# Router logits with the turned tokens as stationary operand, and the experts' scatter as two fp32r products

## The reference

```python
g_logits = xt @ wg + bg                       # xt = RMSNorm(h); 4 groups
e_logits = (xt @ we + be).reshape(n_tok, 4, 8)
e_in = e_logits[tok, argmax(g_logits)]        # 8 experts of the chosen group
top_v, top_i = top_k(e_in, 2)
top_w = softmax(top_v) * g_prob[tok, g_sel]
for e in range(32):
    out += combine[:, e] * ((silu(xt @ w1[e]) * (xt @ w3[e])) @ w2[e])
```

## Time and profile before

| | |
|---|---|
| median of 3 runs | 417.2 us (416.52 to 417.85) |
| the profiled execution | 416.37 us, its span 414.6 us |
| mean granted clock of TensorE | 0.991 |
| PE, PEld busy | 388.9, 269.0 us |
| DVE, ACT, POOL busy | 176.9, 145.4, 12.8 us |
| moved by DMA | 139.88 MB, 337 GB/s over the span |

### The profile page before, as it was taken

The page is one execution under the profiler, slowest core; times in us unless marked ns, Lnnn a source line. Parts: engine busy times, 40 slices in busy tenths (PEclk is TensorE's granted clock), DMA queues, the critical chain, the costliest instruction groups (busy, mean ns, idle before and its releaser), DMA issues.

```text
span 414.6 us, 7327 instructions
## 1 busy us (share of the span) xinstructions
PE 388.9 (94%) x2990; PEld 269.0 (65%) x2990; DVE 176.9 (43%) x340; ACT 145.4 (35%) x285; POOL 12.8 (3%) x33
## 2 busy tenths in 40 slices
PE   7999999999999999999989999999989999979783
PEld 5999988767777777788865555545354646445342
DVE  3847674999898685784263010010102010100203
ACT  6834442638565635442221122121221212211033
POOL 3001000300000000000010000000000000000000
PEclk9999999999999999999999999999999999999897
DMA  8999999643441597569997999999999999999972
GB/s 297 420 417 345 390 397 363 261 152 108 147 154 62 192 344 269 191 243 403 427 419 251 418 430 430 428 411 428 427 427 427 428 428 430 427 428 424 425 326 103
DMA packets 17310, 139.88 MB, mean 337 GB/s; under 512 B 2176, under 2 KB 2560, under 8 KB 5632
## 3 DMA queue, kind: packets, MB, share of 16 engines
q1 hardware_dynamic: 16416, 138.60, 83.0%
q10 hardware_dynamic: 864, 0.84, 0.6%
HBM read 138.38 MB, written 1.05 MB: 336 GB/s over the span
## 4 chain that ended last, share of the span: by engine, by line
PE 47%; issue 46%; DVE 5%; POOL 1%; ACT 0%; POOLq 0%; DVEq 0%
PE bank L1545 5%; PE bank L1547 4%; PE bank L1546 4%; PE bank L1403 4%; PE bank L1404 4%; PE bank L1405 4%; PE bank L1668 2%; PE bank L1666 2%; PE bank L1667 2%; PE bank L1507 1%; PE bank L1533 1%; PE bank L1519 1%; PE bank L1388 1%; PE bank L1565 1%; PE bank L1465 1%
## 5 line engine op out<-in xcount | busy, mean ns | idle before, releaser
L1781 PE MATMUL bank<-ring,kv 128*32 128x512 f32 x512 | 64.1, 607 | 6.9 <-DMA ring<-in_experts 3.9
L464 DVE TENSOR_TENSOR part<-ring,part 128x2048 fp32r<-128x2048 f32 (+1 forms) x26 | 57.4, 2213 | 18.7 <-ACT part L457 18.7
L457 ACT CAST part<-ring 128x2048 fp32r<-128x2048 f32 (+1 forms) x26 | 48.0, 1847 | 31.2 <-DMA ring<-in_front 31.1
L1321 DVE TENSOR_TENSOR kv<-bank,prm 128x512 f32<-128x512 f32 x8 | 5.5, 692 | 109.4 <-PE bank L1749 109.4
L1749 PEld LDWEIGHTS bank<-qcur,h 128*128 128x128 f32 x256 | 32.3, 194 | 28.4 <-issue 28.4
L1749 PE MATMUL bank<-qcur,h 128*128 128x128 f32 x256 | 39.8, 293 | 0.0
L1545 PE MATMUL bank<-part,xhi 128*128 128x512 f32 x96 | 39.2, 408 | 0.0
L1821 PE MATMUL bank<-ring,hidT 128*32 128x256 f32 (+1 forms) x640 | 35.2, 342 | 3.2 <-DMA ring<-in_experts 2.7
L1831 PE MATMUL bank<-gab,vbd 128*128 128x256 f32 (+1 forms) x160 | 36.3, 359 | 1.4 <-ACT gab L911 1.3
L1547 PE MATMUL bank<-part,xlo 128*128 128x512 f32 x96 | 37.6, 391 | 0.0
L1546 PE MATMUL bank<-part,xhi 128*128 128x512 f32 x96 | 37.5, 390 | 0.0
(11 more groups left out here) (243 smaller groups left out, 532.6 us busy)
## 6 DMA issues: line engine op xcount, KB each, us to landing
ring<-in_experts SPq DMA_DIRECT2D x31, 2048.0 KB, 30.9
ring<-in_experts SPq DMA_DIRECT2D x32, 1024.0 KB, 8.4
ring<-in_front SPq DMA_DIRECT2D x28, 1024.0 KB, 5.7
ring<-in_front SPq DMA_DIRECT2D x4, 512.0 KB, 6.9
ring<-in_projs SPq DMA_DIRECT2D x4, 512.0 KB, 5.1
ring<-in_experts SPq DMA_DIRECT2D x4, 512.0 KB, 31.1
ring<-in_front SPq DMA_DIRECT2D x2, 560.0 KB, 8.9
h<-in_x SPq DMA_DIRECT2D x2, 512.0 KB, 3.8
```

The lines of the kernel that those rows point to most:

```text
L457: nc.scalar.copy(high(n, half)[:, 0:c].bitcast(F32R), raw(n, half)[:, 0:c]).then_inc(hi_done, 1)
L464: nc.vector.tensor_tensor(low(n, half)[:, 0:c].bitcast(F32R), raw(n, half)[:, 0:c], high(n, half)[:, 0:c], ALU.subtract).then_inc(split_do ...
L1781: ins = mm(bank[0][CAP * e:CAP * (e + 1)], xgT[:, q, CAP * e:CAP * (e + 1)], expert(j, q, e), start=(q == 0), stop=(q == NQ1 - 1))
```

## The change

The router's product swaps its operands: the turned tokens are stationary (128 columns), the router's 40 real columns move, and the logits come out by token in bank 3 at once. The copy `lgT`, the constant `fold2`, and their semaphores go. All four squares must be done before the first of these matmuls.

The scatter becomes two fp32r matmuls with a stationary operand of zeros and ones: the weight `share` is put on the rows of the second product by ACT, as the high part, and DVE makes the low part, `ylo` (five more instructions a block). DVE's copy of `cmbT` becomes a comparison and a sum. Piece 4 of the second product goes to bank 1. In the tail, the order of second products and scatters changes, DVE takes one of ACT's six squares, and POOL makes the factor of each token tile by itself.

```diff
@@ router, PE
-            pe.wait_ge(ssq_done, NT + 1)
+            pe.wait_ge(ssq_done, NT + 4)
             for k in range(KT):
                 pe.wait_ge(h2T_done[k // 4], 2)
-                ins = mm(bank[0][HD * (k % 2):HD * (k % 2) + HD, 0:T], rw[:, k], h2T[k // 2][:, (k % 2) * T:(k % 2 + 1) * T], start=(k < 2), stop=(k >= KT - 2))
-            ins.then_inc(lgT_full, 1)
-
-            pe.wait_ge(lgT_done, 1)
-            pe.wait_ge(ssq_done, NT + 4)
-            for t in range(NT):
-                ins = mm(bank[3][:, t * RC:(t + 1) * RC], lgT[:, t * P:(t + 1) * P], fold2, start=True, stop=True)
+                for t in range(NT):
+                    ins = mm(bank[3][:, t * RC:(t + 1) * RC], h2T[k // 2][:, (k % 2) * T + t * P:(k % 2) * T + (t + 1) * P], rw[:, k, 0:RC],
+                             start=(k == 0 and t == 0), stop=(k == KT - 1 and t == NT - 1))
             ins.then_inc(logit_full, 1)
@@ router, ACT
-            act.wait_ge(lgT_full, 1)
-            nc.scalar.copy(lgT, bank[0][:, 0:T]).then_inc(lgT_done, 1)
@@ blocks, ACT and DVE
-                nc.scalar.copy(yN[:, columns(p)], second_out(p, slice(0, P))).then_inc(yn_done, 1)
+                nc.scalar.activation(yN[:, columns(p)].bitcast(F32R), second_out(p, slice(0, P)), ACT.Copy, scale=share).then_inc(yn_done, 1)
-                nc.vector.tensor_copy(cmbT, bank[1][:, 0:T]).then_inc(cmb_done, 1)
+                nc.vector.tensor_scalar(cmbT.bitcast(F32R), bank[1][:, 0:T], 0.0, None, ALU.is_gt)
+                nc.vector.tensor_reduce(share, bank[1][:, 0:T], AX.X, ALU.add).then_inc(cmb_done, 1)
@@ blocks, DVE, at the end of through(b)
+                for p in range(NP):
+                    dve.wait_ge(yn_done, b * NP + (p + 1) + 1)
+                    dve.wait_ge(comb_done, b * NP + (p - 2 + 1 + NP))
+                    nc.vector.scalar_tensor_tensor(low_out(p).bitcast(F32R), second_out(p, slice(0, P)), share, yN[:, columns(p)],
+                                                   ALU.mult, ALU.subtract).then_inc(ylo_done, 1)
@@ blocks, PE, combine(p)
+                        pe.wait_ge(ylo_done, b * NP + (p + 1))
                         for t in range(NT):
-                            ins = mm(sum_of_piece(t, p), cmbT[:, t * P:(t + 1) * P], yN[:, columns(p)],
+                            onehot = cmbT[:, t * P:(t + 1) * P].bitcast(F32R)
+                            mm(sum_of_piece(t, p), onehot, yN[:, columns(p)].bitcast(F32R), start=False, stop=False)
+                            ins = mm(sum_of_piece(t, p), onehot, low_out(p).bitcast(F32R),
@@ blocks, PE, order
                     second(1)
                     combine(0)
+                    second(2)
+                    combine(1)
+                    second(3)
                     if j < ROUND - 1:
-                        second(2)
-                        combine(1)
-                        second(3)
                         combine(2)
+                        second(4)
                     else:
-                        combine(1)
-                        second(2)
+                        second(4)
                         combine(2)
-                        second(3)
-                    second(4)
                     combine(3)
                     combine(4)
@@ tail, ACT
             second_copy(blocks, 1)
+            second_copy(blocks, 2)
             last_square(0, 0)
-            last_square(0, 1)
-            second_copy(blocks, 2)
-            last_square(1, 0)
-            last_square(1, 1)
             second_copy(blocks, 3)
             second_copy(blocks, 4)
-            last_square(2, 0)
-            last_square(2, 1)
-            act.wait_ge(rstd_last, 1)
+            for n in (1, 2):
+                for t in range(NT):
+                    last_square(n, t)
+            act.wait_ge(rstd_last, 2)
@@ tail, DVE
+            half_row = last_squares[:, 1, 512:D]
+            step(nc.vector.tensor_copy(half_row, bank[5][:]))
+            step(nc.vector.scalar_tensor_tensor(last_squares[:, 1, 0:512], half_row, 1.0 / D, half_row, ALU.mult, ALU.mult,
+                                                accum_out=stat[:, 13:14]))
+            gain(1, slice(0, 512), half_row, 3 * NT)
...
-            nc.vector.tensor_tensor(stat[:, 28:30], stat[:, 28:30], stat[:, 16:18], ALU.add).then_inc(means_done, 1)
+            for t in range(NT):
+                dve.wait_ge(ssq_done, 3 * NT + 4 + t)
+                nc.vector.tensor_tensor(stat[:, 28 + t:29 + t], stat[:, 28 + t:29 + t], stat[:, 16 + t:17 + t], ALU.add).then_inc(means_done, 1)
@@ tail, POOL
-            nc.gpsimd.tensor_tensor(stat[:, 30:32], stat[:, 28:30], stat[:, 32:34], ALU.pow).then_inc(rstd_last, 1)
+            for t in range(NT):
+                pool.wait_ge(means_done, 2 + t)
+                nc.gpsimd.tensor_tensor(stat[:, 30 + t:31 + t], stat[:, 28 + t:29 + t], stat[:, 32:33], ALU.pow).then_inc(rstd_last, 1)
```

More of the change, by code:

```diff
@@ L119 @@
 K_CAP = K_FOLD + 32
-K_FOLD2 = K_CAP + MAXPASS
-K_CB = K_FOLD2 + RC
+K_CB = K_CAP + MAXPASS
 K_DIST = K_CB + NT * HEADS * 16
@@ L238, in build @@
         last_squares = over("last_squares", [P, NT, D], "ring", 14 * SLOT)
+        act_squares = over("act_squares", [P, NT, D], "ring", 15 * SLOT)
         xgT = kv[:].rearrange("p (k s) -> p k s", k=KT)
-        yN = gab[:].rearrange("p a c -> p (a c)")
+        yN = over("yN", [P, D], "gab")[:]
+        ylo = (over("ylo0", [P, QC], "rw"), over("ylo1", [P, QC], "rw", QC))
+        gflat = gab[:].rearrange("p a c -> p (a c)")
         h2T = [kv[:, 0:512], kv[:, 512:1024], ga, gb]
@@ L245, in build @@
         vflat = vbd[:].rearrange("p g c -> p (g c)")
-        lgT = qcur[:]
         lg, gap1, key1, left, gap2, key2 = [kv[:, i * NT * RC:(i + 1) * NT * RC] for i in range(6)]
-        first, second_of, both = [yN[:, i * NT * RC:(i + 1) * NT * RC] for i in range(3)]
+        first, second_of, both = [gflat[:, i * NT * RC:(i + 1) * NT * RC] for i in range(3)]
         top1, big1, top2, big2, behind, e2, weight, c1, c2, total = [vflat[:, 256 + 16 * i:256 + 16 * i + NT * ROWS] for i in range(10)]
@@ L252, in build @@
         share1, share2 = [vflat[:, i * NT * NE:(i + 1) * NT * NE].rearrange("p (t e) -> p t e", t=NT) for i in range(2)]
-        cmbT = vflat[:, 0:256]
+        cmbT = over("cmbT", [P, T], "vbd")[:]
+        share = stat[:, 41:42]
         hN = vflat[:, 256:512]
@@ L268, in build @@
         fold = con[:, K_FOLD:K_FOLD + 32]
-        fold2 = con[:, K_FOLD2:K_FOLD2 + RC]
         steps_of_cap = con[:, K_CAP:K_CAP + MAXPASS]
@@ L366, in build @@
         h2T_done = [sem(f"h2T_done{i}") for i in range(2)]
-        lgT_full = sem("lgT_full")
-        lgT_done = sem("lgT_done")
         logit_full = sem("logit_full")
@@ L384, in build @@
         yn_done = sem("yn_done")
+        ylo_done = sem("ylo_done")
         gained = sem("gained")
@@ L474, in second_out, with low_out @@
         def second_out(p, rows):
-            return bank[(0, 3)[p % 2]][rows, 0:PIECES[p][1] - PIECES[p][0]]
+            return bank[(0, 3, 0, 3, 1)[p]][rows, 0:PIECES[p][1] - PIECES[p][0]]
+        def low_out(p):
+            return ylo[p % 2][:, 0:PIECES[p][1] - PIECES[p][0]]
         def summed(t, qt):
@@ L694, in _ @@
             nc.gpsimd.tensor_tensor(flat(comb), flat(share1), flat(share2), ALU.add).then_inc(comb_ready, 1)
-            pool.wait_ge(means_done, 2)
-            nc.gpsimd.tensor_tensor(stat[:, 30:32], stat[:, 28:30], stat[:, 32:34], ALU.pow).then_inc(rstd_last, 1)
+            for t in range(NT):
+                pool.wait_ge(means_done, 2 + t)
+                nc.gpsimd.tensor_tensor(stat[:, 30 + t:31 + t], stat[:, 28 + t:29 + t], stat[:, 32:33], ALU.pow).then_inc(rstd_last, 1)
         @block.scalar
@@ L930, in last_square @@
                 act.wait_ge(comb_done, passes * (NP * NB) + (p + 1))
-                nc.scalar.activation(last_squares[:, t, (0, 512, 768)[n]:(512, 768, D)[n]], b, ACT.Square,
+                nc.scalar.activation(act_squares[:, t, (0, 512, 768)[n]:(512, 768, D)[n]], b, ACT.Square,
                                      scale=D ** -0.5, accum_out=stat[:, 12 + NT * n + t:13 + NT * n + t]).then_inc(ssq_done, 1)
@@ L1362, in gain @@
                 nc.vector.tensor_tensor(fin[:, 1, c], sums, fing[:, c], ALU.mult).then_inc(gained, 1)
-            gain(1, slice(0, 512), bank[5][:], 3 * NT + NT)
-            gain(2, slice(512, 768), summed(1, 2), 3 * NT + 2 * NT)
-            dve.wait_ge(ssq_done, 3 * NT + 2 * NT)
+            dve.wait_ge(comb_done, passes * (NP * NB) + 2)
+            half_row = last_squares[:, 1, 512:D]
[3 more added lines that the diff above has]
+            gain(1, slice(0, 512), half_row, 3 * NT)
+            gain(2, slice(512, 768), summed(1, 2), 3 * NT + 3)
             nc.vector.scalar_tensor_tensor(stat[:, 28:30], stat[:, 12:14], EPS, stat[:, 14:16], ALU.add, ALU.add).then_inc(means_done, 1)
-            dve.wait_ge(ssq_done, 3 * NT + 3 * NT)
             dve.wait_ge(means_done, 1)
```

(7 more changed lines are left out.)

## The result

The changed kernel takes 419.96 us (median of 9 runs, 418.44 to 420.34), the kernel before 416.54 in the same comparison: ratio 1.0066, 95% interval 1.0054 to 1.0079. It is slower by 0.66%, outside the 0.3% that can pass for no change. The forecast was 418.3 in a range of 416.5 to 420.2: right in its sign and within the range, 1.7 us short by the medians. The change itself, forecast at +1.1 us, is +3.4 us by the difference of these medians and +2.7 us by the ratio.

The account below looks back on a forecast made before the run. The prediction took DMA's fixed stretch of weight loads, between the router and a tail, to bound the kernel. Router +1.7, blocks zero and tail -0.6 us gave +1.1, from 417.2 to 418.3 us, range 416.5 to 420.2.

Parts of the forecast that it names:

- What bounds the kernel: Whole kernel: 220.5 us until PE has used chunk 0, a fixed 178 us of DMA, a 16 us tail.
- The router's cost to DVE: Router: DVE starts 1.7 us later, from a later first matmul and 32 records at 0.115 us each.
- the identity matmuls: Behind the router on PE: claimed to need less time than DVE up to the mask, so they hold up nothing.
- rival 2: Tail: PE's clock falls to 1.2 GHz in products and scatters, adding 3 us, 421.3 in all; chance 0.12.
- All of the router's loss reaches the end: After the router: the first refill and 72 chunks end 1.7 us later, and the blocks take nothing back.
- Blocks: zero: Blocks: PE saves 1.8 us a block, but a block is 29.7 us of DMA, so the effect is zero.
- Tail: End of the kernel: -0.6 us, between -0.1 if ACT's output decides and -1.2 if DVE's does.
- 1 (weight loads pulled ahead): Router: records cost 0.08 us, DVE starts only 0.65 later, total change about 0, 417.3 us; chance 0.15.
- 3 (the tail gives 2.0): Tail: DVE's extra work hides and PE's whole -2.0 us comes through, with router +1.6: 416.8; chance 0.13.
- 4 (low parts hold up the tail): Tail: DVE's low parts delay scatter 3 by 1 us, tail +0.4, sum +2.1, 419.3 us; chance 0.2.
- Sum: Whole kernel: router +1.7 and tail -0.6 make +1.1 us, median from 417.2 to 418.3; chance 0.4.
- the signs: Profile after: 32 router records of 3.5 to 3.8 us, first refill near 222.2, scatter records x160, longer last-scatter-to-end.

Follow-up runs that it names:

- experiment 2: The changed kernel with the old router put back (copy and fold included), new scatter and tail kept: 416.24 us, ratio 0.9987 to the kernel before.
- experiment 3: The changed kernel with ACT's last square of h using bank 2, so the router need not wait for it: 417.10 us, ratio 1.0005 to before.
- experiment 1: The kernel before with the new router alone, old scatter and tail: 419.69 us, ratio 1.0077 to the kernel before.
- experiment 4: The changed kernel with 128 moving columns instead of 40 in the router's matmuls, wait kept: 417.95 us, ratio 1.0027 to the kernel before.
- experiment 5: The changed kernel with two useless float32 matmuls ahead of the wait for the last square: 418.33 us, ratio 1.0034 to the kernel before.
- experiment 6: The kernel of experiment 2 with tile 1's first tail square back on ACT, DVE's copy and square gone: 415.48 us, ratio 0.9971 to before.
- experiment 10: The changed kernel run unaltered a third time, for a profile in its upper group of times: 421.70 us.

## Why the prediction was right or wrong, point by point

- *What bounds the kernel.* Right. From the first refill to the last wait for weights it is 177.94 us before, 178.10 after, though a block that waits for nothing takes PE 20.9 us now (SiLU at 232.37 and 253.29) in place of 22.1. In the profiles of experiments 2 and 3 the same stretch is 179.0 and 178.9, 1.0 longer; in those of experiments 1, 4, 5 and 6 it is 177.9 to 178.3. SP's last issue stands 146.7 us behind the first refill in experiments 2 and 3 as in after, and the last wait ends on a chunk in both, so the time lies in the transfers behind that issue; why stays open.
- *The router's cost to DVE, +1.7 (1.6 to 2.0).* Measured +1.65 (213.63 - 211.76 - 0.22). The start moved by 0.97 (209.79 - 208.60 - 0.22), said 0.92; the pace was 0.111, the lower bound, said 0.115. The profiles split it in two: from the first transpose to DVE it is 5.13 us before, 5.75 in experiment 3 and 6.78 after, so 0.62 for the records and 1.03 for the wait. By the runs, the wait is experiment 4 less 3, 0.22% or 0.9 us, and the records are 3 less 2, 0.18% or 0.8 us, both with intervals of some 0.6 us to either side.
- *"Behind PE's matmuls are queued the identity matmuls ..., which need less time than DVE does from the logits to the mask, before and after, so they hold up nothing."* This step failed. At 2.4 GHz it holds (experiments 3 to 5: PE waits 0.69 to 0.71 us for the mask). At 1.2 GHz it does not: the identity matmuls take 5.2 us (213.35 to 218.57) where DVE needs 4.1, and PE is 0.84 us late at the mask, of which 0.64 us reaches the first refill. In the long form, where the product itself slows too, the refill is another 1.7 us later (1.87 less the 0.20 of the front). By the ratios, after less experiment 4 is 0.39%, 1.6 us: the part that the forecast lacked. I had looked for the clock only in the tail (rival 2), and not at the place where the change itself makes PE idle and then feeds it 40 columns a weight load.
- *All of the router's loss reaches the end.* Right: refill +2.51, last wait +2.67.
- *Blocks: zero.* Right, and some costs within are as said: 0.47 and 0.48 for copy and low part, 0.12 between the scatter's later records. What PE saves is not: a block is 1.15 us shorter (22.07 to 20.92), said 1.8. A 256-column scatter takes 0.66 us to the next product's start (237.03 to 237.69), said 0.48, because its second record starts 0.22 after the first and the product 0.21 after the last; and PE waits for low parts 2.9 us in eight places. As DMA sets the blocks' time, the error cost nothing there.
- *Tail, -0.6 (-0.1 to -1.2).* Measured -0.77. Less the shift of 2.67, DVE's last three start at 408.56 (said 408.5) and ACT's at 409.07 (said 409.1 to 409.2). PE gained less than said: the last scatter ends at 405.93 (408.60 less 2.67), said 405.4, before 407.39. Experiment 6 shows that DVE's row was the late one, as said: relieved of its square it gives 0.7 us. By the ratio, experiment 2 gives -0.5, by the medians -0.6.
- *Rivals.* 1 (weight loads pulled ahead) is out: the pace is 0.111. 2 (a low clock in the tail's products) did not come: these run at 1.00 in all three profiles of after. The dip of the last block, which before has too, lasted 6.8 us in one of them (experiment 10) and brought PE 1.5 us late to the tail (179.61 against 178.10). 3 (the tail gives 2.0) is out: it gives 0.77, and 1.44 with DVE's square taken off (16.12 against experiment 6's 14.68). 4 (low parts hold up the tail) is out: the first scatter there waits 0.33 us for one.
- *Sum.* +1.1 said; the profile's difference without clock and front is 1.65 + 0.16 - 0.77 = 1.04. The mechanisms of the forecast were right and one term, the clock behind the router, was put at zero. The forecast gave "same" 0.48 and "slower" 0.44; it is slower, by the term that it lacked. That 419.96 still lies within the range is luck: the range reached to 420.2 for rivals that did not come, and two of the nine runs lie above it. Of the signs, 32 records of 3.7 us, 160 scatter records and a longer way from the last scatter to the end (7.9 against 7.2 us) came; the first refill at 223.05 instead of 222.2 was the one that told of the missing part.

## What to carry to other kernels

Count a float32 matmul with few moving columns by its stationary operand (0.111 us a record for 128 columns here): swapping operands to save a copy turned 16 weight loads of 64 columns into 32 of 128 and lost. Where a stretch gets an idle gap and then many weight loads with little moving data, look at the granted clock of the stretch *behind* it, and ask whether what runs there is hidden at half the clock too. A band of run times with two groups is worth a second and third profile.

## What the runs showed of the hardware that was not expected

- A gap of 0.91 us followed by 32 records of 128 stationary and 40 moving columns was followed by a granted clock of 0.50 for 3.4 us (three profiles) or 6.8 us (two), in all five profiles that there are of it. The same gap followed by records of 128 moving columns was not (one profile, six runs within 0.5 us), nor were the 32 records of 40 columns without a gap (two profiles; one of the 22 runs has a time and a mean clock that leave it open). 64 of these without a gap were, for 10.2 us (one profile, four runs).
- Two matmuls of no use (1.0 us) in the gap, or up to 88 unread columns more in each router matmul, made the kernel 1.3 and 1.6 us faster.
- The short dip begins at 213.0 to 213.8 us, the long one at 212.1 to 212.2, behind the same instructions, and the router-alone kernel's runs fall in two groups by that.
